# Moving eighteen conditioning sums into the last two down projections, and the gate rows through HBM

## The reference, cut to what matters

```
mod   = (silu(c) @ w_mod + b_mod)[:, None, :]
mod_c = (silu(c_ctx) @ w_mod + b_mod)[None, None, :]
sh1, sc1, g1, sh2, sc2, g2 = split(mod, 6)
csh1, csc1, ...            = split(mod_c, 6)       # only the first two are used
h  = rmsnorm(x, norm1_g) * (1 + sc1) + sh1
hc = rmsnorm(ctx, norm1_g) * (1 + csc1) + csh1
... retention and attention on h @ w_in and hc @ w_in ...
x = x + g1 * (concat([ret, att]) @ w_out)
h2 = rmsnorm(x, norm2_g) * (1 + sc2) + sh2
x = x + g2 * (square(relu(h2 @ w_ff1)) @ w_ff2)
out = rmsnorm(x, final_norm_g)
```

## Time and profile before

| what | value |
|---|---|
| median of 3 runs | 1186.64 us (1185.91 to 1189.78) |
| the profiled execution's own time | 1183.16 us |
| its span, first to last instruction | 1181.4 us |
| mean granted PE clock | 0.963 |
| PE busy | 1094.8 us (93%) |
| DVE busy | 844.0 us (71%) |
| ACT busy | 596.3 us (50%) |
| POOL busy | 84.6 us (7%) |
| DMA | 192.46 MB, mean 163 GB/s |

### The profile page before, as it was taken

The page is one execution under the profiler, slowest core; times in us unless marked ns, Lnnn a source line. Parts: engine busy times, 40 slices in busy tenths (PEclk is TensorE's granted clock), DMA queues, the critical chain, the costliest instruction groups (busy, mean ns, idle before and its releaser), DMA issues.

```text
span 1181.4 us, 20845 instructions
## 1 busy us (share of the span) xinstructions
PE 1094.8 (93%) x7586; PEld 1002.1 (85%) x7586; DVE 844.0 (71%) x1508; ACT 596.3 (50%) x1018; POOL 84.6 (7%) x99
## 2 busy tenths in 40 slices
PE   3999799899999999976899999999999897999996
PEld 3998799799999889975799999888867686999885
DVE  4895787677888877795489888566778645556554
ACT  4556232455656545436476666555444644445542
POOL 0103142110000000110000000001100100000000
PEclk9998898999999999986999999999999988999998
DMA  8474243168666785990456665644422124666551
GB/s 255 125 213 146 89 143 108 37 215 249 190 188 190 242 277 176 313 345 2 163 158 179 178 182 186 204 140 124 126 71 72 36 75 122 179 180 208 190 185 53
DMA packets 216592, 192.46 MB, mean 163 GB/s; under 512 B 6801, under 2 KB 194321, under 8 KB 216401
## 3 DMA queue, kind: packets, MB, share of 16 engines
q1 hardware_dynamic: 206832, 159.49, 44.9%
q0 software_dynamic: 8512, 31.99, 7.7%
q10 hardware_dynamic: 1184, 0.14, 0.1%
HBM read 190.55 MB, written 1.05 MB: 162 GB/s over the span
## 4 chain that ended last, share of the span: by engine, by line
PE 62%; issue 18%; DVE 10%; DMA 4%; ACT 4%; POOL 1%; DVEq 0%; SPq 0%; POOLq 0%; ACTq 0%
PE ps L539 17%; PE ps L541 17%; PE ps L540 17%; DVE wL L1785 2%; DMA modw<-in_w_mod_t 2%; PE ps L768 1%; DMA raw<-in_a_w_in 1%; PE ps L933 1%; PE ps L754 1%; DMA raw<-in_f_w_up 1%; PE ps L738 1%; DVE cv L1807 1%; ACT wH L1102 1%; PE ps L911 1%; PE ps L823 1%
## 5 line engine op out<-in xcount | busy, mean ns | idle before, releaser
L1785 DVE TENSOR_TENSOR wL<-raw,wH 128x1024 fp32r<-128x1024 f32 x298 | 355.4, 1221 | 117.1 <-ACT wH L1102 115.3
L1102 ACT ACTIVATE wH<-raw 128x1024 fp32r<-128x1024 f32 x298 | 309.4, 1058 | 230.8 <-PE ps L541 206.8
L539 PE MATMUL ps<-yH,wH 128*128 128x256 f32 x704 | 199.1, 283 | 0.3 <-DVE wL L1785 0.3
L540 PE MATMUL ps<-yL,wH 128*128 128x256 f32 x704 | 198.3, 282 | 0.0
L541 PE MATMUL ps<-yH,wL 128*128 128x256 f32 x704 | 198.3, 282 | 0.0
L539 PE MATMUL ps<-xH,wH 128*128 128x256 f32 x512 | 146.5, 286 | 2.4 <-DVE xL L1785 2.3
L540 PE MATMUL ps<-xL,wH 128*128 128x256 f32 x512 | 145.8, 285 | 0.0
L541 PE MATMUL ps<-xH,wL 128*128 128x256 f32 x512 | 145.7, 285 | 0.0
L539 PEld LDWEIGHTS ps<-yH,wH 128*128 128x128 f32 x704 | 132.7, 188 | 0.5 <-DVE wL L1785 0.5
L540 PEld LDWEIGHTS ps<-yL,wH 128*128 128x128 f32 x704 | 132.7, 188 | 0.1
L541 PEld LDWEIGHTS ps<-yH,wL 128*128 128x128 f32 x704 | 132.7, 188 | 0.0
(11 more groups left out here) (385 smaller groups left out, 1873.8 us busy)
## 6 DMA issues: line engine op xcount, KB each, us to landing
raw<-in_f_w_up SPq DMA_DIRECT2D x88, 512.0 KB, 4.7
raw<-in_w_ff SPq DMA_DIRECT2D x64, 512.0 KB, 4.1
modw<-in_w_mod_t POOLq DMA_DIRECT2D x48, 512.0 KB, 5.2
raw<-in_f_w_down SPq DMA_DIRECT2D x44, 512.0 KB, 4.3
raw<-in_a_w_in SPq DMA_DIRECT2D x32, 512.0 KB, 4.9
raw<-in_w_in SPq DMA_DIRECT2D x22, 512.0 KB, 3.8
raw<-in_w_kv SPq DMA_DIRECT2D x16, 512.0 KB, 4.8
raw<-in_a_w_out SPq DMA_DIRECT2D x8, 512.0 KB, 4.2
```

Of the source, the lines that this page charges most:

```text
L539: mm(o, l[0], r[0], start=first, stop=False, skip_group_check=check)
L540: mm(o, l[0], r[1], start=False, stop=False, skip_group_check=check)
L1102: fn(wH[:, c % SPLIT], raw[:, c % RAW], ACT.Copy).then_inc(hi_done, 1)
L1785: return tt(o, x, hi.bitcast(F32), ALU.subtract)
```

## The change

The 64 sums stay, in the same order. Sums 36 to 46 are now in down0 (11 instead of 9), ten are in down1, eight in ff2, and none is in k, v and q. The last 18 tiles (30 to 47) go to a second ring `modw2`, placed 80 KB into the shared area, on tiles that are free by then. `gate1` keeps silu(c) until the end, so the gate of wo_c goes to `gate2` and the gate of ff2 to `gate1`. The two diagonal tiles, PE's products with ones and ACT's copies are gone; a gate column is written to HBM (`gate_store`, 32 bytes from each partition) and read back as one row broadcast to 128 partitions (`gate_load`). The row comes back in the order "p k", so it is read with a stride of 8 elements (`by_tiles`). `modulation` now makes `gs1` alone; `modulation_rest` stands in win, between the seventh and eighth unit's `wL` and `key_rows(0)`; `last_gate` stands behind the loop of ff2. The loops of down1 and ff2 on DVE are written out.

```diff
+MOD_LATE = 30
+MODS_WITH = {"down0": (1, 3, 4, 5, 7, 9, 10, 11, 13, 15, 17), "down1": (0, 1, 3, 5, 7, 9, 11, 13, 15, 17), "ff2": range(2, 18, 2)}
+        modw2, = place(80, ("modw2", [P, MOD_RING, D]))
-            def gate_rows(j):
-                if j == 0:
-                    for g in range(2):
-                        pe.wait_ge(gate_dve, g + 1)
-                        for c in range(2):
-                            last = mm(ps[AUX + 2 * g + c][:], K_["ones"], gate_diag[g][:, c * 512:(c + 1) * 512],
-                                      start=True, stop=True)
-                    last.then_inc(gate_pe, 1)
...
-            token_major("wo_b", X, gate_rows)
+            token_major("wo_b", X, lambda j: turn_added("wo_b", j))
...
@@ POOL
+            def gate_store(g):
+                pool.wait_ge(gate_dve, g + 1)
+                pool.dma_start(gate_hbm[g].rearrange("(p k) -> p k", p=P), gate_cols[:, g]).then_inc(gate_out, 16)
+            def gate_load(g, o):
+                pool.wait_ge(gate_out, 16 * g + 16)
+                pool.dma_start(o[:], gate_hbm[g:g + 1].partition_broadcast(P).rearrange("p a n -> p (a n)")).then_inc(gate_in, 16)
...
-            mod_fetch(44)
+            mod_fetch(46)
             norm("kv")
-            mod_fetch(64)
+            mod_fetch(46)
...
             norm("ctx")
+            pool.wait_ge(x_ready, READY["ctx"] + 4)
+            mod_fetch(56, 40)
             pool.wait_ge(ms_done, STAT["n1"] + 1)
             inverse_root(r4[:]...).then_inc(rstd_done, 2)
+            gate_store(0)
             pool.wait_ge(pw_in, 4)
...
                 inverse_root(st_a[:, t, 1, 0:8], st_a[:, t, 0, 0:8]).then_inc(pw_out, 1)
+            gate_load(0, gate2)
             pool.wait_ge(pw_in, 7)
...
             norm("n2")
+            pool.wait_ge(m_o, RET_H)
+            mod_fetch(64, MOD_TILES)
+            gate_store(1)
+            gate_load(1, gate1)
             pool.wait_ge(unstaged, STAGED["wo_c"] + 4)
             pool.dma_start(rows_f[:], ...).then_inc(final_in, 16)
             norm("fin")
@@ DVE, down
-                    if name == "down0" and j % 2:
+                    if j in MODS_WITH.get(name, ()):
                         mod_sums(1)
-                if name == "down0":
+                if name in MODS_WITH:
                     for j in range(count - SPLIT):
                         body(0, j)
+                    if name == "ff2":
+                        last_gate()
...
                     if c == 0:
+                        if gate is not None:
+                            dve.wait_ge(gate_in, 32)
                         dve.wait_ge(half_done, ...)
...
-                            st.do(tt(tmp, b, gate[:, c * 512:(c + 1) * 512], ALU.mult))
+                            st.do(tt(four(tmp), four(b), by_tiles(gate)[:, 4 * c:4 * c + 4], ALU.mult))
@@ DVE, residual
-                        st.do(tt(s, s, rep(gate[:, bass.ds((i * 4 + j) * 256, 256)], TT), ALU.mult))
+                        for t in range(TT):
+                            sk = s[:, t].rearrange("p (k n) -> p k n", k=2)
+                            st.put(tt(sk, sk, by_tiles(gate)[:, 2 * j:2 * j + 2], ALU.mult))
+                        st.wait(st.n)
@@ DVE
+            def by_tiles(gate):
+                return gate[:].rearrange("p (n k) -> p k n", k=KD)
             def modulation():
-                dve.wait_ge(mod_used, mod_before(MOD_TILES))
-                st.put(tt(modc[:, :, 0], modc[:, :, 0], col("b_mod", 0, 48), ALU.add))
...
-                for g in range(2):
-                    tt(gate_diag[g]..., rep(ident, 8), bc(modc[:, 16 + 24 * g:24 + 24 * g, 0], P), ALU.mult).then_inc(gate_dve, 1)
+            def modulation_rest():
+                dve.wait_ge(mod_used, mod_before(40))
+                tt(gate_cols[:, 0], modc[:, 16:24, 0], col("b_mod", 16, 8), ALU.add).then_inc(gate_dve, 1)
+                st.do(tt(modc[:, 24:40, 0], modc[:, 24:40, 0], col("b_mod", 24, 16), ALU.add))
+                st.put(stt(gs2[:], modc[:, 32:40, 0], 1.0, col("norm2", 0, 8), ALU.add, ALU.mult))
+            def last_gate():
+                dve.wait_ge(mod_used, mod_before(MOD_TILES))
+                tt(gate_cols[:, 1], modc[:, 40:48, 0], col("b_mod", 40, 8), ALU.add).then_inc(gate_dve, 1)
...
-            blocks("k", key_tiles, after=lambda j: query_pair(2 + j) if j < 2 else mod_sums(2))
-            blocks("v", after=lambda j: mod_sums(2))
-            blocks("q", query_tiles, after=lambda j: mod_sums(2))
+            blocks("k", key_tiles, after=lambda j: query_pair(2 + j) if j < 2 else None)
+            blocks("v")
+            blocks("q", query_tiles)
...
-            residual("wo_c", gate1)
+            dve.wait_ge(gate_in, 16)
+            residual("wo_c", gate2)
-            down("ff2", FF2_TILES, gate2)
+            down("ff2", FF2_TILES, gate1)
```

More of the change, by code:

```diff
@@ L223, in build @@
         modc = sb("modc", [P, MOD_TILES, 2])
+        gate_cols = sb("gate_cols", [P, 2, KD])
         gs1 = sb("gs1", [P, KD, 2])
@@ L360, in build @@
         gate_dve = sem("gate_dve")
-        gate_pe = sem("gate_pe")
-        gate_act = sem("gate_act")
+        gate_out = sem("gate_out")
+        gate_in = sem("gate_in")
         out_done = sem("out_done")
@@ L447, in halves, with mod_tile @@
             return x.rearrange("p (n h s) -> p n h s", h=2, s=s)[:, :, odd]
-        gate_diag = [cv[:].rearrange("p a b n -> p (a b n)"), xv[:, 0:4].rearrange("p a n -> p (a n)")]
+        gate_hbm = nc.dram_tensor("gate_rows", (2, D), F32, kind="Internal").ap()
+        def mod_tile(m):
+            return (modw if m < MOD_LATE else modw2)[:, m % MOD_RING]
         r_order = ("up0", "k", "up1")
@@ L599, in token_major @@
                 turns(pe, BLOCKS[name][1], body)
-            def gate_rows(j):
-                if j == 0:
-                    for g in range(2):
-                        pe.wait_ge(gate_dve, g + 1)
-                        for c in range(2):
-                            last = mm(ps[AUX + 2 * g + c][:], K_["ones"], gate_diag[g][:, c * 512:(c + 1) * 512],
-                                      start=True, stop=True)
-                    last.then_inc(gate_pe, 1)
-                if j == 1:
-                    pe.wait_ge(gate_act, 1)
-                turn_added("wo_b", j)
             def down(name, count):
@@ L1612, in _ @@
             band_act()
[L1614 to L1621, removed]
+            added("wo_b", "f1", lambda k: col("f_norm1", k))
             ffn(1)
@@ L1661, in _, with mod_fetch @@
                 pool.dma_start(o[:], a[x].partition_broadcast(P).rearrange("p a n -> p (a n)")).then_inc(cond_in, 16)
-            def mod_fetch(products):
-                while fetched[0] < MOD_TILES and (fetched[0] < MOD_RING or mod_before(fetched[0] - MOD_RING + 1) <= products):
+            def mod_fetch(products, tiles=MOD_LATE):
+                while fetched[0] < tiles and (fetched[0] < MOD_RING or mod_before(fetched[0] - MOD_RING + 1) <= products):
                     m = fetched[0]
@@ L1669, in mod_fetch @@
                         pool.wait_ge(mod_used, mod_before(m - MOD_RING + 1))
-                    pool.dma_start(modw[:, m % MOD_RING], a["w_mod_t"][m * P:(m + 1) * P, :]).then_inc(mod_in[m % MOD_RING], 16)
+                    pool.dma_start(mod_tile(m), a["w_mod_t"][m * P:(m + 1) * P, :]).then_inc(mod_in[m % MOD_RING], 16)
             fetched = [0]
+            def gate_store(g):
[4 more added lines that the diff above has]
+                pool.dma_start(o[:], gate_hbm[g:g + 1].partition_broadcast(P).rearrange("p a n -> p (a n)")).then_inc(gate_in, 16)
             norm("a")
@@ L1802, in mod_sums @@
                         dve.wait_ge(mod_in[m % MOD_RING], 16 * (m // MOD_RING + 1))
-                    w = modw[:, m % MOD_RING]
+                    w = mod_tile(m)
                     o = cv[:].rearrange("p a b n -> p (a b n)") if m < 16 else w
@@ L1909, in body @@
                     if gate is not None:
-                        st.do(tt(s, s, rep(gate[:, bass.ds((i * 4 + j) * 256, 256)], TT), ALU.mult))
+                        for t in range(TT):
+                            sk = s[:, t].rearrange("p (k n) -> p k n", k=2)
+                            st.put(tt(sk, sk, by_tiles(gate)[:, 2 * j:2 * j + 2], ALU.mult))
+                        st.wait(st.n)
                     tt(hc, hc, s, ALU.add).then_inc(unstaged, 1)
-                blocks(name, body, 1 if gate is not None else 0, after=after)
+                blocks(name, body, TT if gate is not None else 0, after=after)
             def added(name, n, gain, after=None):
@@ L2328, in win_dve @@
                 ahead_lo(6, 7)
+                modulation_rest()
                 key_rows(0)
@@ L2436, in modulation @@
             def modulation():
-                dve.wait_ge(mod_used, mod_before(MOD_TILES))
-                st.put(tt(modc[:, :, 0], modc[:, :, 0], col("b_mod", 0, 48), ALU.add))
```

(11 more changed lines are left out.)

## The result

| | before | after |
|---|---|---|
| median of 4 runs, us | 1187.22 (1185.91 to 1189.78) | 1167.12 (1164.31 to 1168.69) |
| ratio | | 0.9828 [0.9809, 0.9846] |
| profiled execution's own time / span, us | 1183.16 / 1181.4 | 1168.48 / 1166.7 |
| mean granted PE clock | 0.963 | 0.965 |

The change is worth 20.1 us by the medians and 14.7 by the two profiled executions (that of before lay 4 us under its median, that of after 1.4 over). The forecast was 6.8, and 1167 is outside its range. Its rivals lie still further off.

What follows compares the result with a forecast made beforehand. PE, busy 93% of the span, was taken to bound the kernel, with waits at q's end and wo_b; 4.9 + 3.5 - 0.1 - 1.5 = 6.8 us off the median 1186.64 gave 1179.8 us, range 1175.5 to 1185.

Steps and rivals of the forecast that it cites:

- step 1: End of q: with the sums out of k, v and q, the attention's first maxima start sooner, 4.9 us off.
- step 3: down0, down1 and ff2: two, ten and eight more sums fit beside PE's work and cost 0.
- step 2: wo_b: without the gate products PE goes straight from block 0 to block 1, 3.5 us off.
- rival B: down1 and ff2: the added sums show, by late tiles holding DVE; 5 us, 1184.8 us in all, chance 0.05.
- Step 4: win: POOL's gate store delays `key_rows` by 4.0 us, covered by DVE's idle behind it; 0.
- Step 5: wo_c: one gate multiply becomes two halves, of which only the last block's pair is in the chain; 0.1 us on.
- Step 6: End of ff2: the last gate's store and load through HBM come late for the multiply, 1.5 us on.
- rival A: Last residual and wo_c: multiplies by the strided gate are slower, 0.54 us each, 2.7 us; 1182.5 us, chance 0.34.
- C: Attention after q: the gain of step 1 doesn't come, 2.8 us are left; 1181.9 us, chance 0.05.
- D: End of ff2: the gate's HBM round trip is slow, gate 15.5 us late; 7.2 us slower, 1193.8 us, chance 0.05.
- E: Somewhere costed at nothing, a tile waited for in order cancels the gain; 1186 us, chance 0.05.

Runs made afterwards that it cites:

- experiment 2: Changed kernel with `mhalf` cut from 32 to 16 columns, so the shared tiles lie at their old addresses; 1178.32 us, ratio 0.9943.
- experiment 8: Changed kernel with `last_gate` behind body 17 of ff2, gate stored as single floats in plain order, `xH` and what follows 64 bytes higher; 1157.43 us, ratio 0.9776.
- experiment 3: Changed kernel with `last_gate` behind body 17 of ff2, inside the loop, instead of behind all 28; 1166.24 us, ratio 0.9843.

## Why the prediction was wrong

**What failed** is not a term of the sum but one that it lacks. The prediction put up0, down0, q, up1, down1 and ff2 at PE's old pace ("this doesn't move, since PE ran q at full pace", in step 1, and 0 in step 3; up0 and up1 it doesn't name). A busy share of 100% at clock 1.00 was read as the pace that PE has; up0 alone then took 116.02 us instead of 120.50, and the six stages together 9.4 us less. The cause is the 64 bytes that `gate_cols` puts ahead of the shared area. It is shown from both sides: alone 0.9906, the change without it 0.9943. The product of the two is 0.985, with some 0.0026 on either side from their intervals; 0.9828 can't be told from it. As times, 11 and 7 of the 20 us.

**Steps 1 and 2 were right.** The maxima start 2.91 us behind PE's end of q instead of 8.42, and instead of 7.63 in the second execution of the kernel before. That is 5.5 or 4.7, where 4.4 to 5.3 had been forecast. The first scores ran at a clock of 1.00 after the short gap, 0.71 us instead of 1.23; the next scores again took 1.23 at 0.50. From PE's end of q to wo_b it is 47.3 and 47.7 us before, 43.0, 41.6 and 43.0 after: step 1 is worth 4.3 to 6.1 by single executions, 4.9 forecast. Line 607 is gone and wo_b gave 3.4 of 3.5. v and q have a DMA share of 0.59 and 0.69 in the windows above; 0.5 had been named.

**Step 3 was right.** down1 with ten sums has PE at 53.00 of 53 and DVE at 43.51, 268 GB/s; forecast 42 of 50 and 290. With the old addresses (experiment 2) down0, down1 and ff2 take 61.52, 61.50 and 89.40 us, as before to 0.01 us, with the sums in them. DVE has no wait for `modw2` in the changed kernel, so rival B falls.

**Step 4 was right.** DVE's idle before `key_rows` in the changed kernel, and what comes behind it:

```profile
804.41 0.29 DVE L2209 TENSOR_TENSOR aqkv<-aqkv,st_a 128x128 f32<-128x128 f32 x1 [2.69 <-POOL st_a L1638]
...
812.76 0.69 DVE L2259 TENSOR_TENSOR wt<-wt,tb 128x512 f32<-128x512 f32 x1 [0.96 <-ACT wt L1378]
```

`key_rows` is 3.2 us late instead of 4.0, since POOL's powers took 2.02 us and not 2.99; the idle behind it shrinks from 4.56 to 0.96, and PE has none.

**Step 5 was mis-sized a little.** From PE's last product of wo_c to its first of ff1 it is 12.25 us before and 12.66 after, 0.4 more instead of 0.1; with the gate in plain order (experiment 8) it is 12.32. So the last block's pair of multiplies, too, is longer by the stride.

**Step 6 was mis-sized**, 2.5 us instead of 1.5. The wait for the gate itself cost 1.0 (PE's first half was done near 1150.7): the store took 1.7 us instead of 2.7, the load 4.1. The Trainium skill ("DMA: Bandwidth & Descriptors", section "Anatomy of one DMA — SWDGE (gpsimd) path") gives 2.0 and 3.2 for the two: near for this store (in experiment 3, amid ff2's loads, it was 3.6 or more), low for the load. The rest is rival A at two thirds of its price: all instructions by the gate are longer.

```profile
L1919 DVE TENSOR_TENSOR stage<-stage,gate x8: 617/696/710, 942.8 to 960.2; 128x256 f32<-128x256 f32 x8
L1900 DVE TENSOR_TENSOR stage<-ps,gate x4: 1056/1063/1157, 1151.7 to 1156.9; 128x512 f32<-128x512 f32 x4
```

A multiply of 512 costs 0.37 us more and one of 256 costs 0.28; I had 0.54. Four make 1.5. The rule of the 16-byte line, "SBUF — State Buffer" in the Trainium skill (section "Door 1: The DMA port swizzle"), agrees in direction; experiment 8, with neighbouring elements and 0.69 us again, shows that it is the stride; experiment 3 had the gate early and kept 1.06 to 1.18. I gave A a chance as an alternative to the forecast, and it was an addition to it.

Rivals C, D and E don't come: the gain of step 1 is there, and from the store's issue to the multiply there are 6.2 us. The forecast's sum, 6.8, and the change timed at the old places, 6.9, agree, in part by luck: step 6 cost 1.0 us more, step 5 0.3 more and step 2 gave 0.1 less, and with step 1 at 4.3 to 6.1 the terms as measured make 4.8 to 6.6. The span of experiment 2 is 4.8 under that of before. All of these lie within its interval, 4.6 to 8.9.

**Open.** What decides between the two paces at 192. How the distance acts: the direction differs between a stage that streams 256 columns of `y` and one that streams 512 of `w`, and no run separates `wH` from `wL`.

The stretch from q's end to up1 takes 91.5 us before, 94.8 with the 64 bytes alone, 95.4 with the weights moved and 83.7 after, so 3 to 4 us of what the layout gives are lost again in the first two. Both parts of the loss occur without the layout. One is the stretch from the first maxima to wo_b, 40.4 us in both, which has 38.8 or 40.1 in unedited executions of the kernel before. The other is the granted clock at the start of wo_b, here with the 64 bytes alone, with the weights moved, in experiment 3, and after:

```profile
567.00:570.00 3.00, 3.00 (x15) 3.00 (x15) 2.40 (x4) 0.00 (x0) 2.26 (x4) 0.50 0.52 165
```
```profile
566.50:569.50 3.00, 3.00 (x15) 3.00 (x16) 2.52 (x4) 0.00 (x0) 2.33 (x4) 0.50 0.34 134
```
```profile
559.50:562.50 3.00, 3.00 (x15) 3.00 (x15) 0.00 (x0) 0.00 (x0) 2.28 (x4) 0.50 0.61 147
```
```profile
559.50:562.50 3.00, 3.00 (x27) 3.00 (x27) 0.00 (x0) 0.00 (x0) 2.24 (x4) 1.00 0.48 142
```

With the 64 bytes alone, wo_b's first 3.6 us ran at 0.50 and wo_b took 1.6 us more; experiment 3, a form of the changed kernel, has it too. Where the clock comes back differs between executions, and what decides it stays open.

## What to carry to other kernels

A new tile of 64 bytes is an edit of every tile allocated behind it. Compare the addresses as well as the instructions, and when a stage changes that no line touched, look at its granted clock first and then count PE's products in equal windows, for a pace shows neither in busy shares nor in the clock. Before a restructuring is credited with a gain, run it with the old addresses and run the addresses alone; an unused tile costs one line, and here it gained more (11 us) than the restructuring (7).

## What the runs showed of the hardware

- At a granted clock of 1.00, with weight loads and products both at 80.00 of 80 us, a product of 256 columns came every 118.3 ns or every 112.8 (up0), by where its operands lie to each other modulo 256 bytes. Of the five distances only 192 brought up0 to 116 us; 0 was worst there and best for the down projections (87.24 us against 88.06 to 89.77 in ff2). At 0 and at 64 `x` and `y` have the same pace: 119.3 and 119.6 ns, 117.1 and 117.3.
- One kernel, unedited, has up1 in 113.31 or 109.08 us at a granted clock of 1.00, so a single profile can mislead by 4 us. ff1 in 93.88 or 92.38 us is the granted clock, 3.4 us at 0.50 or none.
- A stride of 32 bytes in one float32 operand makes a DVE multiply of 512 elements 1.06 us instead of 0.69.
- A store of 4 KB to HBM, issued at the same place in ff2, took 4.2 us to the issue of the load behind it as 128 pieces and 11.9 as 1024.
